# Input projection of an encoder layer: one level of Strassen's scheme in two passes of 768 tokens

## The reference

```python
h = rms_norm(x, norm1) * (1 + scale1) + shift1
p = h @ w_in                      # (tokens, 1024) @ (1024, 5024)
p_rwkv, p_mla, p_gate = jnp.split(p, [RWKV_COLS, RWKV_COLS + MLA_COLS], axis=-1)
y_a = rwkv7_mixer(p_rwkv, ...)    # first step: centred_shift with shift_mu, then kk, decay, a
y_b = mla_mixer(p_mla, ...)
gates = jax.nn.sigmoid(p_gate + b_merge)
x = x + gate1 * ((g_a * y_a + g_b * y_b) @ w_out)
x = x + gate2 * hier_moe(h2, ...)
```

## Time and profile before

| | us |
|---|---|
| median of 3 runs | 2607.88 (2598.62 to 2617.52) |
| the profiled execution, its own time | 2595.92 |
| its span, first to last instruction | 2594.1 |
| `front`: first matmul of the projection, last one | 62.9, 801.1 |
| PE / PEld / DVE / ACT / POOL busy, share of the span | 91% / 72% / 64% / 43% / 30% |

### The profile page before, as it was taken

One profiled execution on the slowest core, in us unless ns is written; L12 is line 12 of the kernel. 1 busy time (PEld: TensorE's weight loads), 2 busy tenths in 40 slices (PEclk: granted clock), 3 DMA queues, 4 the chain that ended last, 5 costly groups with the idle time before them and its releaser, 6 DMA issues. The chain is left out here.

```text
span 2594.1 us, 53583 instructions
## 1 busy us (share of the span) xinstructions
PE 2363.7 (91%) x22387; PEld 1879.8 (72%) x22387; DVE 1653.8 (64%) x2459; ACT 1127.2 (43%) x1945; POOL 770.9 (30%) x511
## 2 busy tenths in 40 slices
PE   3999999999997999899989799998998996989897
PEld 1787777788886888888878666666876884566664
DVE  4744568975663455555467566666886886667664
ACT  3300033344441566656455455553122221666664
POOL 2222244554542445554123200001300000444443
PEclk7999999999998999999989999999999997999998
DMA  7244334434434233222143611104756446999994
GB/s 279 110 138 143 125 121 144 148 134 146 147 140 168 60 97 101 80 77 77 56 129 108 164 32 31 31 13 152 253 161 226 153 144 229 322 348 336 337 312 100
DMA packets 196193, 394.07 MB, mean 152 GB/s; under 512 B 39856, under 2 KB 105168, under 8 KB 182896
## 3 DMA queue, kind: packets, MB, share of 16 engines
q1 hardware_dynamic: 173776, 322.58, 37.1%
q0 software_dynamic: 12960, 36.59, 5.1%
q10 hardware_dynamic: 9216, 31.46, 3.0%
HBM read 294.57 MB, written 106.48 MB: 155 GB/s over the span
## 5 line engine op out<-in xcount | busy, mean ns | idle before, releaser
L99 PE MATMUL ps_in<-h_t_low,w_in_high 128*128 128x512 f32 x960 | 381.4, 397 | 0.0
L100 PE MATMUL ps_in<-h_t_high,w_in_low 128*128 128x512 f32 x960 | 374.2, 390 | 0.0
L101 PE MATMUL ps_in<-h_t_high,w_in_high 128*128 128x512 f32 x960 | 373.9, 389 | 0.0
L99 PEld LDWEIGHTS ps_in<-h_t_low,w_in_high 128*128 128x128 f32 x960 | 180.4, 188 | 47.6 <-issue 9.3
L101 PEld LDWEIGHTS ps_in<-h_t_high,w_in_high 128*128 128x128 f32 x960 | 180.2, 188 | 38.3
L1269 POOL TENSOR_TENSOR wkv_levels<-wkv_nt,level_mask 128x1024 f32<-128x1024 f32 x60 | 140.6, 2363 | 225.5 <-ACT wkv_nt L1214 225.5
L100 PEld LDWEIGHTS ps_in<-h_t_high,w_in_low 128*128 128x128 f32 x960 | 180.5, 188 | 34.8
L506 ACT COPY p_row<-ps_in 128x512 f32<-128x512 f32 x72 | 42.1, 589 | 288.3 <-PE ps_in L101 250.5
L3075 PE MATMUL ps_xy<-w_tile,hidden_turned 128*128 128x512 f32 x272 | 126.5, 608 | 29.3 <-DMA w_tile<-in_w 27.9
L328 POOL CAST w_in_high<-w_in_tile 128x1024 fp32r<-128x1024 f32 x40 | 47.3, 1182 | 348.1 <-PE ps_in L101 346.1
L2962 POOL TENSOR_TENSOR row_gate<-row_gate,latents_then_v 128x1024 f32<-128x1024 f32 x34 | 81.2, 2389 | 183.5 <-ACT row_gate L3153 177.5
(11 more groups left out here) (432 smaller groups left out, 6266.4 us busy)
## 6 DMA issues: line engine op xcount, KB each, us to landing
merged_t<-in_w SPq DMA_DIRECT2D x36, 1024.0 KB, 16.6
w_tile<-in_w SPq DMA_DIRECT2D x34, 1024.0 KB
w_now<-in_w SPq DMA_DIRECT2D x30, 1024.0 KB, 15.3
...
w_in_tile<-in_w_in SPq DMA_DIRECT2D x40, 512.0 KB, 3.7
...
p_t<-p_mixed ACTq DMA_DIRECT2D x24, 512.0 KB, 3.3
...
```

The source lines that it names most:

```text
L99: nc.tensor.matmul(out, w[0], x[1], start=start, stop=False)
L100: nc.tensor.matmul(out, w[1], x[0], start=False, stop=False)
L101: return nc.tensor.matmul(out, w[0], x[0], start=False, stop=stop)
```

## The change

The projection is cut into 40 **slots** g: two passes of 768 tokens (6 token tiles), each over the 20 pairs. A slot is a 2 x 2 block product: two tiles of weights, split in two halves of 512 features (`HF` = 4 blocks of 128), against the pass's tokens, split in two halves of `QT` = 384. By Strassen's scheme (the form with 15 additions) it needs seven block products e of eight; each is 4 x 3 = 12 matmuls of 384 columns. The seven left operands (weights, or sums of them) are split high and low into `w_s`; the seven right operands (`h` blocks, or sums) into `h_hi` and `h_lo`, which now hold one pass.

- POOL, in slots 0 to 27 (`PREPARED`): four sums of 128 x 512 (`first_sums`, `last_sum`) and seven subtractions `low(g, e)` of 128 x 512. ACT makes the seven casts `high(g, e)`, each after product e of the slot before.
- `w` is one buffer for both halves: `load_w(g)` waits for all seven `low` of slot g - 1, and `first_sums(g)` waits for both loads.
- From slot 8 to 19 SP stores each split operand to DRAM (`keep_split`, 512 KB each); in slots 28 to 39 POOL's queue loads it back (`load_kept`) in place of making it, each after product e of the slot before.
- ACT copies product 0 (`keep_first`), and DVE's `take_out` adds the other six out of PSUM: seven operations of up to 384 columns, eleven in the shifted slots of the second pass, where the first half is cut at the border of the two sequences. Six banks turn round; `product(g, e)` waits for `taken_out` of product e + 1 of the slot before.
- `mix_rows` works on 768 columns in two buffers; edge columns go from pass to pass in `edge`. Gates' Tanh is a pass of ACT in place.
- The operand preparation takes two slots a tile: tiles 0 to 4 in slots 8 to 17, tiles 5 to 11 in slots 26 to 39. The second `beta_kappa` and `alpha_rho` of a tile run in the slot after its two.
- Only six tiles of `x` are loaded at first; the others are loaded by SP in slot 18, once the stores of tile 4 are done, squared there, and normalised, turned and modulated in slot 19; sums and lows of the second pass run on DVE in slots 19 and 20 (`block_sum`, `low_h`, each 128 x 1536).
- At the start SP issues the first `w_ada` tile, then all bias rows, then the other three tiles; DVE does `add_rows(0)`, `add_rows(1)`, the mean squares of six tiles at once, three `normalise`, `add_rows(2)`, three `normalise`, `add_rows(3)`.
- Slots 0 to 7 carry the late `w_ada` tiles, one each.

```diff
+PASSES = 2
+QT = 384
+PASS = 2 * QT
+TP = PASS // P
+PAIRS = (N_SHIFTED + N_GATES) // 2
+TILE_ORDER = (0, 1, 2, 3, 4, 5, 6, 7, 12, 13, 8, 9, 10, 11) + tuple(range(14, N_SHIFTED + N_GATES))
+KEPT = 8
+OPERANDS_AT = 8
+PRODUCTS = 7
+HF = DF // 2
...
+    SLOTS = PASSES * PAIRS
...
+    PREPARED = PAIRS + KEPT
+    TILES_AT = ((OPERANDS_AT, 0, TP - 1), (PAIRS + 6, TP - 1, TT))
...
+    BANKS = 6
...
         w = s.sb("w_in_tile", [P, 2, DF, P])
-        w_hi, w_lo = ([s.sb(f"w_in_{n}{b}", [P, DF, P], F32R) for b in range(2)] for n in ("high", "low"))
-        row = s.sb("p_row", [P, 2, TOK + 3])
-        mix = s.sb("p_mixed", [P, W])
+        sums = s.sb("w_in_sums", [P, 2, HF, P])
+        w_s = s.sb("w_in_split", [P, PRODUCTS, 2, HF, P], F32R)
+        w_kept = w_s[:].rearrange("p e s f c -> p e (s f c)")
+        first_product = s.sb("p_first", [P, QT])
...
-            def load_w(i, b):
-                sp.wait_ge(w_split[b], i)
-                sp.dma_start(w[:, b], dram["w_in"][2 * i + b]).then_inc(w_loaded[b], 16)
+            def load_w(g):
+                for b in range(2):
+                    if g >= 1:
+                        sp.wait_ge(i_["split"], PRODUCTS * g)
+                    tile = TILE_ORDER[2 * (g % PAIRS) + b]
+                    sp.dma_start(w[:, b], dram["w_in"][tile]).then_inc(w_loaded[b], 16)
+
+            def keep_split(g, e):
+                sp.wait_ge(i_["split"], PRODUCTS * g + e + 1)
+                sp.dma_start(dram["w_in_kept"][g - KEPT, e], w_kept[:, e].bitcast(F32)).then_inc(kept_out[e], 16)
 
...
                 if t < NEED + 2:
-                    sp.wait_ge(o["turned"], DF * (t - NEED + 1))
+                    sp.wait_ge(o["h_lo"], PRODUCTS)
                 else:
                     sp.wait_ge(o["parts_full"], t - 1)
                 sp.dma_start(late[t % 2], dram["w_ada"][t]).then_inc(late_in[t % 2], 16)
...
             sp.dma_start(c_rows[:], dram["c"][:, :]).then_inc(o["c_in"], 16)
+            sp.dma_start(early[:, 0], dram["w_ada"][0]).then_inc(ada_in[0], 16)
             for t in range(NEED):
+                load_bias(t)
+            for t in range(1, NEED):
                 sp.dma_start(early[:, t], dram["w_ada"][t]).then_inc(ada_in[t], 16)
-                load_bias(t)
...
+            for g in range(SLOTS):
+                t, second = operand_tile(g)
+                if g + 1 < PREPARED:
+                    load_w(g + 1)
+                if g == 0:
+                    load_late(NEED)
+                    load_late(NEED + 1)
+                if 1 <= g <= OPERANDS_AT:
...
+                if ending(g) is not None:
+                    for d in range(2):
+                        store_operands(ending(g), d)
+                        sp.wait_ge(out_stored[d], 16 * ending(g) + 16)
+                    for u in range(TP, TT):
+                        sp.dma_start(x[:, u - TP], dram["x"][P * u:P * u + P, :]).then_inc(x_in[u], 16)
+                for e in range(PRODUCTS):
+                    if KEPT <= g + 1 < PAIRS:
+                        keep_split(g + 1, e)
+                if g + 1 == OPERANDS_AT:
                     sp.wait_ge(o["parts_full"], MOD_TILES)
-                    sp.dma_start(spread[:], dram["spread_heads"][:, :, :]).then_inc(m["consts_in"], 16)
-            store_operands(TT - 1)
+                    sp.dma_start(spread[:], dram["spread_heads"][:, :, :]).then_inc(m["spread_in"], 16)
+            for d in range(2):
+                store_operands(TT - 1, d)
             for d in range(2):
                 sp.wait_ge(out_stored[d], 16 * TT)
 
         @block.gpsimd
...
+            def high(e):
+                for b in range(2):
+                    pool.wait_ge(w_loaded[b], 16)
+                nc.gpsimd.tensor_copy(w_s[:, e, 0], weight_source(e)).then_inc(i_["hi_ready"], 1)
+
+            def low(g, e):
+                if g == 0:
+                    high(e)
+                pool.wait_ge(i_["hi_ready"], PRODUCTS * g + e + 1)
+                nc.gpsimd.tensor_tensor(w_s[:, e, 1], weight_source(e), w_s[:, e, 0].bitcast(F32), ALU.subtract).then_inc(i_["split"], 1)
+
+            def first_sums(g):
+                for b in range(2):
+                    pool.wait_ge(w_loaded[b], 16 * g + 16)
+                nc.gpsimd.tensor_tensor(sums[:, 0], w[:, 1, 0:HF], w[:, 1, HF:DF], ALU.add).then_inc(i_["sum_ready"], 1)
+                pool.wait_ge(i_["sum_ready"], 4 * g + 1)
+                nc.gpsimd.tensor_tensor(sums[:, 1], sums[:, 0], w[:, 0, 0:HF], ALU.subtract).then_inc(i_["sum_ready"], 1)
+                nc.gpsimd.tensor_tensor(w[:, 1, 0:HF], w[:, 0, 0:HF], w[:, 1, 0:HF], ALU.subtract).then_inc(i_["sum_ready"], 1)
+                pool.wait_ge(i_["sum_ready"], 4 * g + 3)
+
+            def last_sum(g):
+                nc.gpsimd.tensor_tensor(w[:, 0, HF:DF], w[:, 0, HF:DF], sums[:, 1], ALU.subtract).then_inc(i_["sum_ready"], 1)
+                pool.wait_ge(i_["sum_ready"], 4 * g + 4)
+
+            def load_kept(g, e):
+                pool.wait_ge(full, PRODUCTS * (g - 1) + e + 1)
+                pool.dma_start(w_kept[:, e], dram["w_in_kept"][g % PAIRS - KEPT, e]).then_inc(kept_in[e], 16)
 
...
+            first_sums(0)
+            for e in range(PRODUCTS):
+                low(0, e)
+                if e == 4:
+                    last_sum(0)
...
+                if g + 1 < PREPARED:
+                    first_sums(g + 1)
+                    for e in range(3):
+                        low(g + 1, e)
+                if PREPARED <= g + 1 < SLOTS:
...
+                    alpha_rho(t, 0)
+                if PREPARED <= g + 1 < SLOTS:
+                    for e in range(3, 5):
+                        load_kept(g + 1, e)
...
+                        if e == 4:
+                            last_sum(g + 1)
+                if t is not None and not second:
...
+            def product(g, e, between=None):
+                p = g // PAIRS
+                if g < PREPARED:
+                    pe.wait_ge(i_["split"], PRODUCTS * g + e + 1)
+                else:
+                    pe.wait_ge(kept_in[e], 16 * (g - PREPARED) + 16)
+                if g % PAIRS == 0:
+                    pe.wait_ge(o["h_lo"], PRODUCTS * p + e + 1)
+                if e == PRODUCTS - 1:
+                    pe.wait_ge(i_["first_kept"], g + 1)
+                elif g >= 1:
+                    pe.wait_ge(i_["taken_out"], evicted(g - 1, e + 1))
+                if (g, e) == (0, 4):
+                    pe.wait_ge(o["h_act"], len(TURNS) // 2)
+                    pe.wait_ge(o["h_dve"], len(TURNS) // 2)
+                out = bank(g, e)
+                for k in range(HF):
+                    mm = split_product(nc, out, (w_s[:, e, 0, k], w_s[:, e, 1, k]), (h_hi[:, e, k], h_lo[:, e, k]),
+                                       start=(k == 0), stop=(k == HF - 1))
+                    if between is not None:
...
+            def keep_first(g):
+                act.wait_ge(full, PRODUCTS * g + 1)
+                if g >= 1:
+                    act.wait_ge(i_["taken_out"], evicted(g - 1, 4))
+                nc.scalar.copy(first_product[:], bank(g, 0)).then_inc(i_["first_kept"], 1)
+
+            def high(g, e):
+                if g >= PREPARED:
+                    return
+                act.wait_ge(full, PRODUCTS * (g - 1) + e + 1)
+                if KEPT <= g - 1 < PAIRS:
+                    act.wait_ge(kept_out[e], 16 * (g - KEPT))
+                if e in (0, 4, 6):
+                    act.wait_ge(w_loaded[int(e == 6)], 16 * g + 16)
                 else:
...
+            def take_out(g, e):
+
+                dve.wait_ge(full, PRODUCTS * g + e + 1)
+                if e in (1, 4):
+                    dve.wait_ge(i_["first_kept"], g + 1)
                 else:
-                    nc.vector.tensor_scalar(mix[:, 0:TOK], row[:, b, 0:TOK], 0.5, 0.5, ALU.mult, ALU.add).then_inc(mixed, 1)
+                    dve.wait_ge(i_["taken_out"], evicted(g, {2: 1, 3: 2, 5: 3, 6: 2}[e]))
+                if e in (1, 2) and g >= 1:
+                    dve.wait_ge(mixed, 2 * g - 2 + e)
+                first, second = (row_part(g, b, 1) for b in range(2))
+                if e == 1:
+                    ins = V.tensor_tensor(first, bank(g, e), first_product[:], ALU.add)
+                if e == 5:
+                    ins = V.tensor_tensor(first, bank(g, e), first, ALU.add)
+                if e in (2, 3, 4, 6):
+                    for to, at, n in pieces(g, 0):
+                        part = slice(at, at + n)
+                        here = row[:, int(e != 4), to:to + n]
+                        if e == 2:
+                            ins = V.tensor_tensor(here, bank(g, e)[:, part], first[:, part], ALU.add)
+                        if e == 3:
+                            V.tensor_tensor(second[:, part], bank(g, e)[:, part], here, ALU.add)
+                        if e == 4:
+                            ins = V.tensor_tensor(here, bank(g, e)[:, part], first_product[:, part], ALU.add)
```

(18 more changed lines are left out.)

690 lines of the change are left out of this document (424 added, 266 removed).

## The result

The changed kernel takes 2829.69 us (median of 4 runs, 2820.97 to 2833.51) against 2606.53 (2598.62 to 2617.52) of the kernel before, run beside it: ratio 1.0836, 95% interval 1.0804 to 1.0869. It is slower, by 223 us; 2755 were forecast, in a range of 2630 to 2840. The last product of the input projection is issued at 1006.3 us, where it was at 801.1: 205 of the 225 us are lost there, the rest behind it.

What follows compares the result with a forecast made beforehand. It took TensorE to bound the kernel before, POOL's weight path the changed one: 80 + 143 + 102 + 336 + 220 + 72 = 953 us against 801.5, +152, and 3 behind; 2755 us forecast, range 2630 to 2840.

Steps and rivals of the forecast that it cites:

- Rival 3: Whole projection: TensorE keeps the pace, with POOL's weight cycle at some 16 us; -80 us, 2516; chance 0.07.
- Rival 1: POOL's cycle without VectorE's work added: slots 8 to 17, 26 and 27 at 21.7 us; some 2665; chance 0.20.
- Rival 2: Stores ahead of load_w cost 2.5 us a slot, and kept weights load late; 2790 to 2835 us; chance 0.17.
- the change of passes: Slots 18 to 20: normalised at 34, turns 10, sums, lows and casts 16, the rest 10; 72 us.
- The start: Start and slot 0: scale at 41.5 us, 14.5 earlier, and slot 0 ending at 80 (bounds 70 and 90).
- Slots 1 to 7 and 21 to 25: POOL's weight cycle of 20.3 us, including 5.1 of load wait, sets these slots: 143 and 102 us.
- The mixings fall mostly into the load's wait: Shifted slots: VectorE's mixings, 2 x 2.3 us a slot, run mostly while POOL waits for its weight load.
- the engines' sum decides: Slots with operand preparation: POOL's and VectorE's work add up; slots 8 to 11 29.8 us, 12 to 17 26.1 each.
- The check that the forecast rested on: Four pairs of the kernel before: VectorE's and POOL's work summed to 152.5 us against 153.2 taken, so they add up.
- Slots 26 and 27: Weight work and operand preparation together, counted like slots 8 to 11: 29.8 us each.
- Kept slots: Slots 28 to 39, without weight work on POOL: 28 to 31 at 21.1 us, 32 to 39 at 17.0; together 220.
- Behind `front`: After the last product: rates, beta_kappa and a store cost 3 us more, and nothing after front changes.

Runs made afterwards that it cites:

- e3: The changed kernel without the four sums of weight blocks on POOL, plain blocks in their place: 2714.45 us in one run.
- e4: The changed kernel with split weights stored and read back from slot 1 on instead of slot 8 (KEPT = 1): 2791.68 us, ratio 1.0690.
- e8: The changed kernel with slot 0's weights used in all slots, no weight work after it: 2682.45 us in one run, last product at 804.7 us.
- e11: The changed kernel with no stores in slots 8 to 18 and weights prepared again in slots 28 to 38 (KEPT = 19): 2909.13 us in one run.
- e9: The changed kernel with the first mean of squares, root and inverse taken by three tiles of x instead of six: 2830.08 us, ratio 1.0840.
- e10: The changed kernel with the bias rows asked for behind their w_ada tiles again, as in the kernel before: 2836.26 us, ratio 1.0861.
- e2: The changed kernel with the two scalar_tensor_tensor of every shifted row's mixing left out on DVE: 2769.95 us in one run.
- e6: The changed kernel without preparing the second pass's activations, the first pass's being multiplied again: 2863.02 us in one run.
- e5: The kernel before with only the eight bias rows moved up the queue, behind the first w_ada tile: 2605.39 us, ratio 0.9987.

## Why the prediction was right, and where its terms were off

**Direction and mechanism** were right: POOL's weight path paces the prepared slots, TensorE waits between them and is full inside, and the scheme's saving on TensorE never reaches the end. e3, e4 and e8 show it, each from another side. Rival 3 (TensorE keeps the pace) is out by e8. Rival 1 (slots 8 to 17 at 21.7) is out by their 27.2 us, though the sum of the engines is not what fills them, as told below. Rival 2 (kept weights late) is half true: stores cost 1.2 us a slot (e11), while its second part, late reads, is absent; the 74.1 us of L446 are POOL waiting for TensorE.

**The size** was not right. 2830 us lies outside the 2700 to 2800 that the forecast claimed for its own mechanism, 10 us inside the range, and by the number in the band of rival 2 (2790 to 2835), of whose costs only the 12 us of stores in slots 8 to 17 are there. The whole was 75 us under, from terms that err on both sides. Two steps of the sum don't follow either: the parts of the change of passes (34, 10, 16, 10) make 70 and not 72, and 2751 by the profiled execution's own time is 2763 for the median, by the 12 us named beside it, where 2755 was put down.

- **The start, 80 against 109.** The step that failed is the one from "with the bias first and two `add_rows` ahead of the squares" to "scale at 41.5". It left out that one mean waits for all six squares, and that six normalisations and the third `add_rows` stand on DVE before the last: 39.58 to 54.50 us. e9 gives 6.3 back; e10 shows that the bias move had nothing to give while that wait stands. The rest of slot 0 took 53.6 us from the scale on, where 38.5 were forecast. POOL stands 24.5 us in it for ACT, whose casts for slot 1 are behind those of `h` in its program; what share that has was not tried, so that this half of the miss stays open.
- **Slots 1 to 7 and 21 to 25, 245 against 273.** The cycle itself was exact (20.3; e2 measured 20.3). "The mixings fall mostly into the load's wait" failed: products 1 to 6 run while POOL waits for its load, so that the rows are complete, and the mixings begin, just when POOL starts again (both at 205.57 us). That is 2.3 us a slot.
- **Slots 8 to 17, 276 against 272.5**: right by luck, since "the engines' sum decides" did not hold. POOL never waits for DVE there. It works 213.9 us (the windows above) where 18.6 a slot were counted, so that DVE's 7.5 to 11.3 us a slot lengthen its work by only 2.8. The rest is waiting, 4.1 us a slot for the load and 1.6 for the casts, which the forecast had left out. With the work these make 271.4 of the 272.5 us (waits of the kernel after, 268 to 540 us):

```profile
POOL w_in_sums L434 <- DMA w_in_tile<-in_w_in: 41.3, 10, 8.1
POOL w_in_split L429 <- ACT w_in_split L671: 16.2, 16, 1.8
```

  The gate slots' 26.0 us without the stores (e11) are near their 26.1 in the same way, with waits of 22.1 and 20.7 us in those ten slots. TensorE stands in slots 8 to 17 for 37.4 us for ACT's part of the operand preparation and 17.5 for POOL's subtraction. The check that the forecast rested on, pairs 8 to 11 of the kernel before, could not tell a sum from TensorE's own pace: TensorE was busy 98% of them, and POOL waited for it (waits of the kernel before, 353 to 506 us):

```profile
POOL w_in_high L328 <- PE ps_in L101: 36.1, 4, 13.0
```

- **The change of passes, 72 against 93.** Without its work the three slots take 71.2 (e6); it costs 21.9. These are its steps, in the kernel after:

```profile
569.52 0.17 DVE L951 TENSOR_SCALAR rms_parts<-rms_parts 128x6 f32<-128x6 f32 x1 [18.64 <-ACT front_area L741]
...
579.41 2.07 DVE L960 TENSOR_SCALAR front_area<-front_area,rms_parts 128x1024 f32<-128x1024 f32 x3
...
601.90 7.63 DVE L977 TENSOR_TENSOR front_area<-front_area 128x1536 f32<-128x1536 f32 x3
...
619.18 8.01 DVE L981 TENSOR_TENSOR h_t_low<-front_area,h_t_high 128x1536 fp32r<-128x1536 f32 x3
```

  The mean was taken 32 us into slot 18, but the last tile was normalised only 43.6 us into it, where 34 was forecast: on DVE the last gate passes of slot 18, which wait for ACT, and two additions of slot 19 stand between. What follows took 49.5 us where 38 were left, for sums and lows are 2.5 to 2.7 us each beside POOL against 1.75 alone, and POOL's weights for slot 20 come behind. Which share each has was not tried.
- **Slots 26 and 27, 60 against 38.** An oversight: in slot 27 POOL prepares nothing, since slot 28 is kept. The two were counted like 8 to 11.
- **Kept slots, 220 against 221**, and 0.174 us a matmul: as forecast. Slots 28 to 31 take 24 and 15.9 us in turn, 19.9 in the mean against 21.1.
- **Behind `front`, 3 against 20**: not foreseen. DVE's `rates` and `beta_kappa` of the last tile now run to 1015.9 us, 9.6 after the last product, where the kernel before had ended them at 803.6. The rest is the scan, from 28 us after the last product to the query projection; first the kernel before, then after:

```profile
829.10:1294.20 465.10, 424.96 (x12728) 392.88 (x12726) 241.47 (x459) 275.20 (x528) 207.44 (x108) 0.98 0.27 78
```

```profile
1034.30:1517.20 482.90, 437.21 (x12776) 403.61 (x12772) 244.98 (x462) 275.17 (x529) 207.39 (x108) 0.95 0.28 80
```

  It is the same work at a granted clock of 0.95 in place of 0.98. e8, whose projection ran at a full clock for long, has 0.95 too, and e5, a kernel before in all but eight small loads, 0.97. So neither the clock of the projection nor its length explains it. From the last product to the query projection the changed kernel and all its variants take 509 to 520 us, the kernel before 493 and e5 499. The cause stays open.
